# Two layers of a hybrid trunk on one core: layers written out, modulation moved into branch C, output product by tiles, first stage by feature halves

## The chip, the core and the metric

The kernel runs on one core of a Trainium2 chip. The metric is the time of one execution in microseconds (us); lower is better. Engines are named as the profile names them: PE (TensorE, with PEld for its weight loads), DVE (VectorE), ACT (ScalarE), POOL (GpSimd), SP (SyncE, which here only issues DMAs). One run of each kernel is profiled: its span is from the first to the last instruction.

## The reference, cut to what matters

640 tokens (four tiles of 128 latent tokens and one tile of 128 context tokens), 1024 features, two layers. Each layer does

```python
mod_ctx = silu(c_ctx) @ w_mod[l] + b_mod[l]          # for the context tile
mod_lat = silu(c) @ w_mod[l] + b_mod[l]              # for the four latent tiles
shift, scale, gate = split(mod, 3)
u = layer_norm(x) * (1 + scale) + shift
parts = split_columns(u @ w_in)                      # q, k, v, z of A and C, all of B, merge gates
ya, yw, ym = attention A, windowed attention C, two-directional mLSTM B
merged = sum(sigmoid(g_b) * ((y_b * silu(z_b)) @ w_branch[b]) for the 3 branches)
h = alpha * x + gate * (merged @ w_out)
x = layer_norm(h) * ln_g + ln_b
```

All is float32. `mod` depends on the conditioning and the layer alone, not on x.

## The kernel before, in words

**Tiles.** `T` = 5 token tiles, tile 4 (`LT`) is the context. `act_T` holds the modulated input u, features on partitions, as a rounded part (index 0) and a remainder (index 1). Every weight product is three fp32r products (rounded x rounded, rounded x remainder, remainder x rounded), so each of the eight feature blocks of a chunk of 512 output columns costs 3 matmuls of 512 columns for each tile: 24 a tile, 120 a chunk.

**Weights.** A "piece" is two feature blocks of a chunk, 512 KB. SP loads pieces into a ring of three buffers `raw`; POOL writes the rounded part (`tensor_copy`, L654) and the remainder (`tensor_tensor`, L656) into a ring of two buffers `wsp`; PE (`product`, L703) uses a piece for all five tiles, then takes the next. ACT does the rounding of the four pieces of A's z. The table `Pieces` fixes the order, `PsumPlan` which PSUM bank each result takes; an instruction waits for counts of semaphores `bank_full` and `bank_done`.

**A layer.** Both layers are one loop body (`Fori`). It begins with the modulation: `modulation(n, k)` (L688) multiplies two columns `csil` (silu of the two conditionings) by 512 columns of `w_mod`, 8 feature blocks for each of chunks 0 to 3 (0, 1 shift; 2, 3 scale), straight from `raw`. DVE adds the bias (L1442); 16 small transposes put it into columns `modc`. DVE normalises x in `xh` (L1431 to L1447), PE transposes each tile (`xT`, L743), DVE and ACT modulate it (L1468, L1145), ACT rounds (L1149), DVE takes the remainder (L1458, `u_ready`). Then the products kv, A's q, transposes of k, A's z, transposes of q and z, attention A (`for s in range(STEPS)`, a software pipeline over 32 pairs of head and tile), A's merge products, the same for C, then B, and last the transposes of `merged` and the output product. In steps 0 to 15 of C's loop one `modulation` of chunks 4 and 5 (the gate) stands in each step.

**Output.** The output product goes chunk by chunk over all five tiles: half 0 of all tiles, then half 1. For each tile DVE multiplies by the gate (L1934), adds alpha x (L1953), takes statistics (L1959, L1964), subtracts the mean and multiplies by the gain (L1940); POOL makes the reciprocal root (L642); ACT scales (L1396); POOL adds the bias (L671); for tile 4 DVE does the last step (L1970). SP stores the tiles to the outputs, from which the second layer reads them again for its residual.

**The meeting.** At the end of a layer every engine drains and waits (`meet`), SP waits for all stores, clears all semaphores and lets all go on:

```python
                for name in at_end:
                    sp.wait_ge(at_end[name], 1)
                sp.sem_clear(range(bank_full[0].num, at_end["pool"].num + 1))
                sp.wait_ge(stored, 16 * (4 + 6 + T))
```

## Time and profile before

| what | value |
|---|---|
| time, median of 3 runs | 1812.54 us (1806.18 to 1815.93) |
| time of the profiled execution | 1812.43 us |
| its span | 1810.6 us, 21331 instructions |
| granted clock of PE, mean | 0.957 |
| busy: PE, DVE, ACT, POOL | 1632.6, 792.2, 475.8, 611.7 us |
| chain that ended last | PE 76%, DVE 10%, issue 4%, ACT 4%, DMA 2% |

PE is nearly always the engine that the others wait for. The share of busy time by itself says little here, as a slowly running PE is busy too. What is worth reading is where PE is not fed: the page's slices, and the timeline at the start, at the turn between the layers and at the end.

### The profile page before, as it was taken

To read this page: it belongs to the slowest core of one execution; us is meant where nothing else is said; L and a number is where in the kernel's file an instruction comes from. 1 tells how busy PE (TensorE), PEld (TensorE's weight loads), DVE (VectorE), ACT (ScalarE), POOL (GpSimd) and SP (SyncE) were. 2 spreads that over 40 slices of the span, in tenths; PEclk is the share of its full clock that TensorE was granted. 3 is DMA by queue.
4 is the path that set the end of the run, shared out by engine and by line. 5 is a ranking of instruction groups with operands and counts; after the bars stand their busy time and mean duration, and the time that the engine had idled before them with its cause. 6 is when DMAs were issued, how large, how long until landed. Compare 5 with 4: busy or idle time off the path is not lost.

```text
span 1810.6 us, 21331 instructions
## 1 busy us (share of the span) xinstructions
PE 1632.6 (90%) x8235; PEld 1250.8 (69%) x8235; DVE 792.2 (44%) x1456; ACT 475.8 (26%) x1111; POOL 611.7 (34%) x351
## 2 busy tenths in 40 slices
PE   4798899999899999999658979999998999999994
PEld 0487678884588887787505867788746888877874
DVE  2348740356612434323633587304465234252255
ACT  0223740135600133301102237401345001332011
POOL 0254005520044443253512540154210544423535
PEclk8899999998999999999869989999999999999997
DMA  7421002212112222141054310022130222211411
GB/s 259 131 83 58 1 12 71 81 47 85 36 58 82 59 71 64 35 152 59 35 179 128 85 47 1 13 81 78 39 95 26 70 82 59 71 53 47 151 59 58
DMA packets 75874, 131.34 MB, mean 73 GB/s; under 512 B 16044, under 2 KB 20544, under 8 KB 75716
## 3 DMA queue, kind: packets, MB, share of 16 engines
q1 hardware_dynamic: 74728, 124.15, 22.6%
q10 hardware_dynamic: 1040, 5.77, 0.8%
q8 instruction: 68, 1.11, 0.3%
q14 instruction: 38, 0.31, 0.1%
HBM read 123.61 MB, written 8.92 MB: 73 GB/s over the span
## 4 chain that ended last, share of the span: by engine, by line
PE 76%; DVE 10%; issue 4%; ACT 4%; DMA 2%; SPq 2%; POOL 2%; POOLq 0%; ACTq 0%; DVEq 0%
PE pb L718 55%; PE pb L743 4%; PE pb L897 3%; PE pb L696 3%; PE pb L854 2%; DMA raw<-in_w_mod 2%; PE pb L816 2%; PE pb L934 1%; PE pb L827 1%; PE pb L823 1%; DVE rtmp L1553 1%; DVE tokq L1538 1%; SPq L567 1%; POOL rstd L642 1%; POOL xh L671 1%
## 5 line engine op out<-in xcount | busy, mean ns | idle before, releaser
L718 PE MATMUL pb<-wsp,act_T 128*128 128x512 f32 x4080 | 950.3, 393 | 9.2 <-issue 9.2
L718 PEld LDWEIGHTS pb<-wsp,act_T 128*128 128x128 f32 x4080 | 769.5, 189 | 176.9 <-issue 17.2
L654 POOL CAST wsp<-raw 128x1024 fp32r<-128x1024 f32 x152 | 163.0, 1072 | 1102.2 <-PE pb L718 898.2
L656 POOL TENSOR_TENSOR wsp<-raw,wsp 128x1024 fp32r<-128x1024 f32 x160 | 390.6, 2441 | 34.1 <-ACT wsp L1167 21.9
L718 PE MATMUL pb<-wsp,yT 128*128 128x512 f32 x720 | 169.9, 395 | 0.0
L696 PE MATMUL pb<-raw,csil 128*2 128x512 f32 x192 | 104.8, 669 | 59.8 <-DMA raw<-in_w_mod 57.1
L718 PEld LDWEIGHTS pb<-wsp,yT 128*128 128x128 f32 x720 | 135.4, 188 | 32.5
L1914 DVE SCALAR_TENSOR_TENSOR mt<-tg,pb 128x512 f32<-128x512 f32 x40 | 27.4, 685 | 260.2 <-PE pb L718 259.4
L1387 ACT ACTIVATE tg<-pb 128x512 f32<-128x512 f32 x60 | 36.0, 600 | 363.7 <-PE pb L718 363.7
L696 PEld LDWEIGHTS pb<-raw,csil 128*2 128x2 f32 x192 | 12.6, 88 | 122.9 <-DMA raw<-in_w_mod 80.0
L1235 ACT ACTIVATE pr<-pb,nm 128x640 f32<-128x640 f32 (+2 forms) x128 | 91.2, 713 | 2.0 <-DVE nm L1605 2.0
L1914 DVE SCALAR_TENSOR_TENSOR merged<-tg,pb 128x512 f32<-128x512 f32 x20 | 13.7, 687 | 148.8 <-PE pb L718 148.8
L854 PE MATMUL pb<-ident,pr 128*128 128x128 f32 x480 | 74.7, 276 | 1.5 <-ACT pT L1272 1.2
L1635 DVE TENSOR_SCALAR pr<-pr,rden 128x640 f32<-128x640 f32 (+2 forms) x128 | 70.4, 550 | 4.5
L816 PE MATMUL pb<-kT,qT 128*128 128x320 f32 x256 | 56.3, 343 | 9.6 <-ACT prc L1213 7.3
L1605 DVE TENSOR_REDUCE nm<-pb 128x1 f32<-128x640 f32 x64 | 52.5, 820 | 27.3 <-PE pb L816 27.2
L854 PEld LDWEIGHTS pb<-ident,pr 128*128 128x128 f32 x480 | 54.0, 142 | 4.1 <-issue 2.7
L1608 DVE TENSOR_REDUCE nmx<-pb 128x1 f32<-128x384 f32 (+1 forms) x64 | 39.7, 621 | 39.0 <-PE pb L831 38.6
L816 PEld LDWEIGHTS pb<-kT,qT 128*128 128x128 f32 x256 | 39.7, 197 | 21.5 <-issue 9.6
L1918 DVE TENSOR_TENSOR merged<-merged,mt 128x512 f32<-128x512 f32 x40 | 51.5, 1287 | 1.4
L1145 ACT ACTIVATE utmp<-pb,modc 128x128 f32<-128x128 f32 x40 | 15.1, 457 | 119.7 <-PE pb L743 119.1
L1262 ACT COPY pT<-pb 128x512 f32<-128x512 f32 x64 | 37.6, 587 | 31.6 <-PE pb L854 29.7
(242 smaller groups left out, 1637.8 us busy)
## 6 DMA issues: line engine op xcount, KB each, us to landing
raw<-in_w_in SPq DMA_DIRECT2D x112, 512.0 KB, 3.6
raw<-in_w_mod SPq DMA_DIRECT2D x48, 512.0 KB, 4.3
raw<-in_w_branch SPq DMA_DIRECT2D x24, 512.0 KB, 3.5
raw<-in_w_out SPq DMA_DIRECT2D x16, 512.0 KB, 3.5
out<-xh SPq DMA_DIRECT2D x10, 512.0 KB
raw<-in_w_in SPq DMA_DIRECT2D x16, 256.0 KB, 3.3
xh<-out SPq DMA_DIRECT2D x2, 2048.0 KB, 8.7
xh<-in_x_sample ACTq DMA_DIRECT2D x1, 2048.0 KB, 8.6
```

The lines of the kernel that those rows point to most:

```text
L654: pool.tensor_copy(hi, raw[:, p % 3, :, 0:width]).then_inc(pool_step, 1)
L656: pool.tensor_tensor(lo, raw[:, p % 3, :, 0:width], hi.bitcast(F32), ALU.subtract)\
L696: mm = pe.matmul(pb[0:2, psum.bank(key), :], csil[:, k, :], raw[:, p % 3, k % 2, :], start=(k == 0), stop=(k == KD - 1))
L718: mm = pe.matmul(dst, lhs(a, k, t), wsp[:, piece % 2, w, j, 0:width], start=(k == 0 and n == 0), stop=(i == count - 1 and j == 1 and n == 2))
L743: mm = pe.transpose(pb[:, b, tile_cols(i % 4)], src(i), ident[:, :])
L816: mm = pe.matmul(pb[:, b + i, 0:320], q, kT[:, kv, a, i * 320:(i + 1) * 320], start=(a == 0), stop=(a == 1))
L854: mm = pe.transpose(pb[:, psum.bank((br, "PT", s)), tile_cols(i)], pr[:, (s + 2) % 3, tile_cols(i)], ident[:, :])
L897: mm = pe.matmul(pb[r, psum.bank(key), (2 * hh + lo) * P:(2 * hh + hi) * P], v_of, pT[:, g % 2, place_of, 2 * e + lo:2 * e + hi, :] .rearr ...
L1235: act.activation(dst, src, ACT.Exp, bias=nm[:, s % 4:s % 4 + 1], accum_out=lsum[:, s % 4:s % 4 + 1]).then_inc(*done((br, "S", s)))
L1605: dve.tensor_reduce(nm[:, o], pb[:, b:b + 2, 0:320], AX.XY, ALU.max, negate=True)\
L1635: dve.tensor_scalar(p, p, rden[:, o], None, ALU.mult).then_inc(p_ready, 1)
L1918: ins = dve.tensor_tensor(merged[:, t, cs], merged[:, t, cs], mt[:, t % 2, :], ALU.add)
```

## The change

1. The two loop passes are written out, each with its own semaphores; the meeting is gone, and the second layer's work follows the first's on each engine as its own waits allow.
2. Modulation: only chunks 0 to 3 of the first layer are made at the start, from 16 buffers `stage`, loaded by SP and ACT. The other eight chunks stand in branch C's loop: six in the first layer (four of them the second layer's shift and scale), 24 steps with two feature blocks in each; two in the second layer, 8 steps. A block's product is no longer one matmul of 512 columns with 2 stationary columns, but four of 128 columns with 32 stationary columns, each into its own 32 partitions of PSUM; the bias is a product with `ident`. The gate is broadcast from `mrow` by 16 matmuls of 128 columns, before by 4 of 512.
3. The output product is done for tiles 0 to 2 (both halves), then 3 and 4. Its eight pieces, and the second layer's kv and q pieces, stay resident in `slots`. In the first layer DVE normalises each finished tile twice (the layer's own norm, and the next layer's), ACT writes the normalised input into `xn`, PE transposes it, and the next layer's kv and q are multiplied tile by tile, kv of tile t before the transposes of t+1.
4. The first layer's start goes by halves of the features: chunks 0 and 2 give modulation of blocks 0 to 3, then half of kv's product, then chunks 1 and 3, blocks 4 to 7 and the other half.
5. The transposes of k stand inside z's product, behind its third piece. POOL's remainder of a piece is made by two instructions of half the width. In the second layer ACT does the rounding of the four q pieces too.

```diff
+START_CHUNKS = (0, 2, 1, 3)
+LATE_CHUNKS = (((1, 0), (1, 2), (1, 1), (1, 3), (0, 4), (0, 5)), ((1, 4), (1, 5)))
+MOD_FROM = 2
+OUT_SLOTS = (("A1", "A2", "M1", "M2"), ("Y1", "Y2", "w0", "w1"))
+KV_SLOTS = ("T1", "T2", "A1", "A2")
+Q_SLOTS = ("M1", "M2", "w0", "w1")
+Z_SLOTS = ("T1", "T2", "w0", "w1")
+
+OUT_FIRST = (0, 1, 2)
...
+def out_calls(l):
+
+    if l == 0:
+        return [(hf, OUT_FIRST) for hf in range(2)] + [(hf, (3, 4)) for hf in range(2)]
+    return [(hf, OUT_FIRST) for hf in range(2)] + [(hf, (t,)) for t in (3, 4) for hf in range(2)]
...
-            with sp.Fori(0, DEPTH) as l:
...
+            for l in range(DEPTH):
+                here[0] = l
...
-                for name in at_end:
-                    sp.wait_ge(at_end[name], 1)
-                sp.sem_clear(range(bank_full[0].num, at_end["pool"].num + 1))
-                sp.wait_ge(stored, 16 * (4 + 6 + T))
-                sp.sem_clear(stored)
-                sp.drain().then_inc(go_on, 1)
...
+                    load_stage(0)
+                    for p in range(3):
+                        load_piece(p)
+                    load_stage(2)
+                    load_small(0)
...
+                for j in range(2):
+                    ins = pool.tensor_tensor(lo[:, j, :], raw[:, p % 3, j, 0:width], hi[:, j, :].bitcast(F32), ALU.subtract)
+                ins.then_inc(raw_used, 1)
...
+            kv, q, z = chunk(1, "kv"), chunk(1, "A", "q"), chunk(1, "A", "z")
+            split(kv[0])
+            split(kv[1])
+            of_out(0, 0)
+            split(kv[2])
+            of_next(1, 0)
+            of_out(0, 1)
+            split(kv[3])
+            of_next(1, 1)
+            of_out(0, 2)
+            split(q[0])
+            of_next(1, 2)
+            split(q[1])
...
-                    mm = pe.matmul(pb[0:2, psum.bank(key), :], csil[:, k, :], raw[:, p % 3, k % 2, :],
-                                   start=(k == 0), stop=(k == KD - 1))
-                    if k == KD - 1:
-                        mm.then_inc(*full(key))
-                    elif k % 2:
-                        mm.then_inc(mod_used, 1)
...
+                def modulation(b, k, src):
+
+
+                    for q in range(4):
+                        mm = pe.matmul(pb[32 * q:32 * q + 32, b, 0:P], csil[:, k, :], src[:, tile_cols(q)],
+                                       start=(k == 0), stop=False)
+                    return mm
...
-                for n in range(4):
-                    for k in range(KD):
-                        modulation(n, k)
-                acquire("modT")
-                for n in range(4):
-                    wait_done(pe, ("mod", n))
-                for i in range(2 * KD):
-                    mm = pe.transpose(pb[:, 6, 2 * i:2 * i + 2], modrow[:, tile_cols(i)], ident[0:2, 0:2])
-                mm.then_inc(*full("modT"))
-
-                for t in range(T):
-                    pe.wait_ge(xn_ready, t + 1)
-                    transpose_blocks(("xT", t), lambda i: xh[:, t, tile_cols(i)], KD)
-
-
-                project(("kv",), tile_ready=lambda t: pe.wait_ge(u_ready, t + 1))
...
+                    start_chunk(0)
+                    pe.wait_ge(xn_ready[0], T)
+                    for k in range(4):
+                        turn_input(k)
+                    start_chunk(1)
+                    turn_chunk(("modT", 0), 0)
+                    turn_chunk(("modT", 1), 1)
+                    project(("kv",), part=(0, 1), tile_ready=lambda t: inputs_ready(0))
+                    start_chunk(2)
+                    start_chunk(3)
+                    turn_chunk(("modT", 2), 2)
+                    turn_chunk(("modT", 3), 3)
+                    for k in range(4, 8):
+                        turn_input(k)
+                    project(("kv",), part=(2, 3), tile_ready=lambda t: inputs_ready(1))
+                    project(("A", "q"))
...
+                    project((br, "z"), after=keys)
...
-                        if br == "C" and s < 2 * KD:
-                            modulation(4 + s // KD, s % KD)
+                        if br == "C":
+                            late_step(s)
...
-                    project(("out", hf), tile_ready=(lambda t: wait_done(pe, ("mT", t))) if hf == 0 else None)
-                meet(pe, "pe", l)
...
+                def turn_next(t):
+                    pe.wait_ge(xn_ready[here[0]], t + 1)
+                    transpose_blocks(("xT", t), lambda i: xn[:, tile_cols(i)], KD)
+
+                def first_turned(i, t):
+                    if (l, i, t) == (0, 2, T - 1):
+                        here[0] = l + 1
+                        turn_next(0)
+                        here[0] = l
+
+                calls = out_calls(l)
+                for n, (hf, tiles) in enumerate(calls):
+                    project(("out", hf), tiles=tiles, tile_ready=(lambda t: wait_done(pe, ("mT", t))) if hf == 0 else None,
+                            after=first_turned if n == len(calls) - 1 else None)
+                if l + 1 < DEPTH:
+                    here[0] = l + 1
+                    for t in range(T):
+                        project(("kv",), tiles=(t,), by_tile=True, tile_ready=lambda t: pe.wait_ge(u_ready[1], t + 1))
+                        if t + 1 < T:
+                            turn_next(t + 1)
+                        project(("A", "q"), tiles=(t,), by_tile=True)
...
+                    normalised(0)
+                    hi_piece(q)
+                    hi_piece(q + 1)
+                    modulated(0)
+                    normalised(1)
+                    hi_piece(q + 2)
+                    hi_piece(q + 3)
+                    of_kv(0)
+                    modulated(1)
...
+                def mean(t):
+
+                    dve.wait_ge(dve_step[l], ends[1, t])
+                    step(dve.bn_aggr(out=mv[:, t, :], in_=stats[:, t, :, :].rearrange("p a b -> p (a b)")))
+                    dve.tensor_scalar(ve[:, t:t + 1], mv[:, t, 1:2], EPS, None, ALU.add).then_inc(ln_var[l], 1)
                     dve.scalar_tensor_tensor(out=xh[:, t, :], in0=xh[:, t, :], scalar=mv[:, t, 0:1],
                                              in1=lnrow[:, 0, :], op0=ALU.subtract, op1=ALU.mult)\
-                        .then_inc(centred, 1)
-
-
-                for i in range(4):
-                    wait_done(dve, ("gate", i))
-                order = [(hf, t) for hf in range(2) for t in range(T)]
-                aggregated = 0
-                gated(*order[0])
-                for n, (hf, t) in enumerate(order):
-                    cs = slice(hf * HALF, (hf + 1) * HALF)
-                    wait_done(dve, ("out", hf, t))
-                    added = marked(dve.scalar_tensor_tensor(out=xh[:, t, cs], in0=xh[:, t, cs], scalar=ALPHA,
-                                                            in1=ot[:, t % 2, :], op0=ALU.mult, op1=ALU.add))
-                    if hf and t:
-                        dve.wait_ge(dve_step, aggregated)
-                        centre(t - 1)
-                    dve.wait_ge(dve_step, added)
-                    counted = marked(dve.bn_stats(out=stats[:, t, hf, :], in_=xh[:, t, cs]))
-                    if n + 1 < len(order):
-                        gated(*order[n + 1])
-                    if hf:
-                        dve.wait_ge(dve_step, counted)
-                        aggregated = marked(dve.bn_aggr(out=mv[:, t, :],
-                                                        in_=stats[:, t, :, :].rearrange("p a b -> p (a b)")))
-                dve.wait_ge(dve_step, aggregated)
-                centre(LT)
-                dve.wait_ge(rstd_ready, 3 + T + LT)
-                dve.wait_ge(centred, T)
-                dve.scalar_tensor_tensor(out=xh[:, LT, :], in0=xh[:, LT, :], scalar=rstd[:, LT:LT + 1],
-                                         in1=lnrow[:, 1, :], op0=ALU.mult, op1=ALU.add).then_inc(context_ready, 1)
-                meet(dve, "dve", l)
+                        .then_inc(centred[l], 1)
+
+                def scaled(t):
+
+                    dve.wait_ge(ln_rstd[l], t + 1)
+                    dve.wait_ge(centred[l], t + 1)
+                    dve.scalar_tensor_tensor(out=xh[:, t, :], in0=xh[:, t, :], scalar=rstd[:, t:t + 1],
+                                             in1=lnrow[:, 1, :], op0=ALU.mult, op1=ALU.add).then_inc(x1_ready[l], 1)
+
+                def next_mean(t):
+
+                    dve.wait_ge(x1_ready[l], t + 1)
+                    for i in range(2):
+                        ins = dve.bn_stats(out=stats2[:, t, i, :], in_=xh[:, t, i * HALF:(i + 1) * HALF])
+                    step(ins)
+                    step(dve.bn_aggr(out=mv2[:, t, :], in_=stats2[:, t, :, :].rearrange("p a b -> p (a b)")))
+                    dve.tensor_scalar(ve2[:, t:t + 1], mv2[:, t, 1:2], EPS, None, ALU.add).then_inc(xn_var[1], 1)
+
+                def next_shift(t):
+                    dve.wait_ge(xn_rstd[1], t + 1)
+                    dve.scalar_tensor_tensor(out=nmr[:, t:t + 1], in0=mv2[:, t, 0:1], scalar=-1.0,
+                                             in1=rstd2[:, t:t + 1], op0=ALU.mult, op1=ALU.mult).then_inc(next_ready[1], 1)
+
+                def modulated(t):
+                    w = 1 if t == LT else 0
+                    wait_full(dve, ("xT", t), 1)
+                    if t >= 2:
+                        dve.wait_ge(u_ready[1], t - 1)
+                    src = pb[:, use(("xT", t), 1)[0]:use(("xT", t), 1)[0] + 2, :].rearrange("p b (n i) -> p (b n) i", i=P)
+                    for k in range(KD // 2):
+                        ins = dve.tensor_scalar(utmp[t % 2][:, k, :], src[:, k, :], modc[:, KD + k, w:w + 1],
+                                                modc[:, k, w:w + 1], ALU.mult, ALU.add)
+                    ins.then_inc(u_half[1], 1)
+
+                def remainder(t):
+                    wait_done(dve, ("xT", t), 1)
+                    dve.tensor_tensor(act_T[:, 1, :, tile_cols(t)], utmp[t % 2][:, :, :],
+                                      act_T[:, 0, :, tile_cols(t)].bitcast(F32), ALU.subtract).then_inc(u_ready[1], 1)
...
```

The first place is PE at the turn between the layers. Before, the transposes of `merged` and all of the output product end the loop body (the 240 matmuls are both halves), and behind them PE leaves the pass by way of the meeting (L511):

```order
L718 MATMUL pb<-wsp,yT 128x512 x60
L743 MATMUL pb<-ident,merged 128x128 x40
L718 MATMUL pb<-wsp,act_T 128x512 x240
L511 REGISTER_ALU
L682 REGISTER_ALU
L682 COMPARE_AND_BRANCH
```

Now the end of the first layer's output product (tiles 3 and 4, half 1), the transposes of the first normalised tile, and kv, the next transposes and q of the second layer, tile by tile:

```order
L942 MATMUL pb<-slot_Y_137,act_T 128x512 x12
L942 MATMUL pb<-slot_Y_138,act_T 128x512 x12
L942 MATMUL pb<-wsp,act_T 128x512 x12
L967 MATMUL pb<-ident,xn 128x128 x8
L942 MATMUL pb<-wsp,act_T 128x512 x12
L942 MATMUL pb<-slot_T_131,act_T 128x512 x6
L942 MATMUL pb<-slot_T_132,act_T 128x512 x6
L942 MATMUL pb<-slot_A_133,act_T 128x512 x6
L942 MATMUL pb<-slot_A_134,act_T 128x512 x6
L967 MATMUL pb<-ident,xn 128x128 x8
L942 MATMUL pb<-slot_M_135,act_T 128x512 x6
L942 MATMUL pb<-slot_M_136,act_T 128x512 x6
```

The modulation is gone from this place, and the products of the second layer stand directly behind the first's.

The second place is DVE from the statistics of tile 2 on, in the same stretch: what stands between the third tile's statistics and the first remainder (L2438) that kv of tile 0 waits for.

```order
L2422 SCALAR_TENSOR_TENSOR nmr<-mv_77,rstd_79 128x1
L2415 BN_STATS stats_76<-xh 128x6 x2
L2417 BN_AGGR mv_77<-stats_76 128x2
L2418 TENSOR_SCALAR ve_78<-mv_77 128x1
L2385 TENSOR_TENSOR ot<-pb,gate_bc 128x512 x2
L2391 SCALAR_TENSOR_TENSOR xh<-xh,ot 128x512
L2393 BN_STATS stats<-xh 128x6
L2391 SCALAR_TENSOR_TENSOR xh<-xh,ot 128x512
L2393 BN_STATS stats<-xh 128x6
L2422 SCALAR_TENSOR_TENSOR nmr<-mv_77,rstd_79 128x1
L2432 TENSOR_SCALAR utmp_129<-pb,modc 128x128 x4
L2438 TENSOR_TENSOR act_T<-utmp_129,act_T 128x8x128
```

Before, nothing of the next layer stood in this stretch; the last rows of a layer were

```order
L1959 BN_STATS stats<-xh 128x6
L1964 BN_AGGR mv<-stats 128x2
L1939 TENSOR_SCALAR ve<-mv 128x1
L1940 SCALAR_TENSOR_TENSOR xh<-xh,mv,lnrow 128x1024
L1970 SCALAR_TENSOR_TENSOR xh<-xh,rstd,lnrow 128x1024
```

What moved is that the modulation of tile 0 now stands behind the next norm's statistics of tiles 0 to 2 and behind half 0 of tiles 3 and 4.

The third place is PE inside branch C of the first layer, two steps near the loop's start; `raw,csil` and `bmod,ident` are the modulation's products. Before:

```order
L823 MATMUL pb<-kT,qT 128x128 x2
L827 MATMUL pb<-kT,qT 128x384 x2
L831 MATMUL pb<-masks 128x128 x2
L854 MATMUL pb<-ident,pr 128x128 x4
L696 MATMUL pb<-raw,csil 2x512
L823 MATMUL pb<-kT,qT 128x128 x2
L827 MATMUL pb<-kT,qT 128x256 x2
L831 MATMUL pb<-masks 128x128
L854 MATMUL pb<-ident,pr 128x128 x3
L696 MATMUL pb<-raw,csil 2x512
```

Now:

```order
L1092 MATMUL pb<-kT,qT 128x128 x2
L1096 MATMUL pb<-kT,qT 128x384 x2
L1100 MATMUL pb<-masks 128x128 x2
L1123 MATMUL pb<-ident,pr 128x128 x4
L898 MATMUL pb<-raw,csil 32x128 x8
L1092 MATMUL pb<-kT,qT 128x128 x2
L1096 MATMUL pb<-kT,qT 128x256 x2
L1100 MATMUL pb<-masks 128x128
L1123 MATMUL pb<-ident,pr 128x128 x3
L898 MATMUL pb<-raw,csil 32x128 x8
L905 MATMUL pb<-bmod,ident 32x128 x4
```

Each product of 512 columns (one feature block a step) has become four of 128 columns, eight a step (two blocks), and a chunk ends with four more for its bias.

## Rows read from the trace of the kernel before

**Rows 1.** Waits of PE over the span: us in total, times, longest.
```profile
...
PE pb L696 <- DMA raw<-in_w_mod: 57.1, 17, 30.9
PE pb L743 <- DVE zt L1567: 13.5, 2, 6.8
...
```

**Rows 2.** Timeline: both output products, kv of the second layer: start us, us.
```profile
...
834.25 55.98 PE L718 MATMUL pb<-wsp,act_T 128*128 128x512 f32 x238 [0.67 <-issue]
...
977.96 2.47 PE L718 MATMUL pb<-wsp,act_T 128*128 128x512 f32 x5 [4.16 <-issue]
...
1733.26 54.68 PE L718 MATMUL pb<-wsp,act_T 128*128 128x512 f32 x240 [0.77 <-issue]
...
```

**Rows 3.** Timeline behind the last output product of the first layer: start us, us, engine.
```profile
...
885.29 0.69 DVE L1934 TENSOR_TENSOR ot<-pb,gate_bc 128x512 f32<-128x512 f32 x1 [14.48 <-PE pb L718]
886.01 0.69 DVE L1953 SCALAR_TENSOR_TENSOR xh<-xh,ot 128x512 f32<-128x512 f32 x1
886.74 0.69 DVE L1959 BATCH_NORM_STATS2 stats<-xh 128x6 f32<-128x512 f32 x1
...
887.94 0.20 DVE L1964 BATCH_NORM_AGGREGATE mv<-stats 128x2 f32<-128x12 f32 x1
...
888.67 0.14 DVE L1939 TENSOR_SCALAR ve<-mv 128x1 f32<-128x1 f32 x1
888.73 1.27 DVE L1940 SCALAR_TENSOR_TENSOR xh<-xh,mv,lnrow 128x1024 f32<-128x1024 f32 x1
...
892.07 1.53 POOL L642 TENSOR_TENSOR rstd<-ve,half_neg 128x1 f32<-128x1 f32 x1 [1.66 <-DVE ve L1939]
...
893.57 2.34 POOL L671 TENSOR_TENSOR xh<-xh,lnrow 128x1024 f32<-128x1024 f32 x1
...
894.41 2.05 DVE L1953 SCALAR_TENSOR_TENSOR xh<-xh,ot 128x512 f32<-128x512 f32 x1
...
916.56 6.03 DVE L1431 BATCH_NORM_STATS2 stats<-xh 128x6 f32<-128x512 f32 x10 [6.71 <-issue]
...
972.74 1.06 PE L743 MATMUL pb<-ident,xh 128*128 128x128 f32 x8 [1.00 <-ACT act_T L1149]
...
977.89 1.37 DVE L1468 TENSOR_SCALAR utmp<-pb,modc 128x128 f32<-128x128 f32 x4
...
979.17 1.22 DVE L1458 TENSOR_TENSOR act_T<-utmp,act_T 128x1024 fp32r<-128x1024 f32 x1
979.42 1.05 ACT L1149 CAST act_T<-utmp 128x1024 fp32r<-128x1024 f32 x1
```

**Rows 4.** Chain that ended last, end of the second layer.
```profile
...
1803.75 3.35 DVE xh L1970
```

**Rows 5.** Timeline: ACT reads the last kv tile of the first layer.
```profile
...
105.26 0.37 ACT L1154 COPY kvt<-pb 128x256 f32<-128x256 f32 x1 [0.71 <-PE pb L718]
...
```

**Rows 6.** Busy times by stretch, at the start and late in branch C.
```profile
...
40.00:45.00 5.00, 4.09 (x10) 0.74 (x11) 0.57 (x2) 0.00 (x0) 0.00 (x0) 1.00 0.88 283
...
475.00:485.00 10.00, 8.38 (x69) 6.14 (x68) 8.19 (x29) 7.81 (x24) 0.00 (x0) 1.00 0.00 0
...
```

**Rows 7.** Timeline of PE inside branch C.
```profile
...
420.87 1.09 PE L863 MATMUL pb<-pTc,kv 128*64 128x128 f32 x16
421.89 1.02 PE L696 MATMUL pb<-raw,csil 128*2 128x512 f32 x2
...
```

**Rows 8.** Page, part 5: the costliest groups, GpSimd's.
```profile
...
L654 POOL CAST wsp<-raw 128x1024 fp32r<-128x1024 f32 x152 | 163.0, 1072 | 1102.2 <-PE pb L718 898.2
L656 POOL TENSOR_TENSOR wsp<-raw,wsp 128x1024 fp32r<-128x1024 f32 x160 | 390.6, 2441 | 34.1 <-ACT wsp L1167 21.9
...
```

**Rows 9.** Page, part 6: DMA issues.
```profile
...
raw<-in_w_mod SPq DMA_DIRECT2D x48, 512.0 KB, 4.3
...
```

**Rows 10.** Page, part 3: DMA queues.
```profile
...
q8 instruction: 68, 1.11, 0.3%
q14 instruction: 38, 0.31, 0.1%
...
```

1494 lines of the change are left out of this document (953 added, 541 removed).

## Prediction

> **What bounds the kernel now.** I read the waits of PE first. Of all its waits one stands out: 57.1 us for `w_mod`, in the two modulation stages; the next, 13.5 us, is for the gating of z [rows 1]. So elsewhere PE is fed, and time can come only from the stages without weight products and from a change in PE's own work. How long the first kind is, the timeline shows, once one sees where PE's product ends: DVE begins with tile 0 of the last half at 885.29, but PE still has four tiles to go. The first layer's output product runs from 834.25 for 55.98 us, to 890.2, and kv of the second layer starts at 977.96 [rows 2]: 87.7 us, in which PE makes only modulation and transposes. The second output product ends at 1733.26 + 54.68 = 1787.9 [rows 2], the last DVE step at 1807.1 [rows 4], and the span at 1810.6: 22.7 us. At the start the last tile of kv is read at 105.26 [rows 5]; what is left, two layers of some 800 us of dense work, the change mostly keeps.
>
> **Turn.** Removed: meeting, reload of x, modulation, all 87.7 us. Added to PE at this place: only the transposes of five tiles, 5 x 1.06 = 5.3 us, already there before [rows 3]. The question is how long PE waits for DVE. I lay it out from the start of the output product. A matmul takes 54.68/240 = 0.228 us [rows 2], 24 take 5.5. In half 1, tiles 0 to 2 are done at 30.1, 31.4 and 32.8 us, all at 54.7. From 30.1 DVE has, up to the first remainder (the order above): 5 gate products at 0.69, 5 additions and 5 statistics at 0.69 each, 3 means (0.20 + 0.14 + 1.27), 3 final scalings at 1.27, 3 next statistics (2 x 0.60, from 6.03/10, + 0.34), shifts 0.4, half a modulation 1.37, ACT's rounding 1.05, remainder 1.22 [rows 3]. That is 3.5 + 6.9 + 4.8 + 3.8 + 4.6 + 0.4 + 1.4 + 1.1 + 1.2 = 27.7 us, so u of tile 0 at 57.8. Two things come on top. POOL's roots take 1.53 us, and that for tile 2 stands behind the next layer's root of tile 1: 2 x 1.53 with hand-overs, 4.5 us of waiting. And DVE is held while POOL works: `xh<-xh,ot` takes 2.05 instead of 0.69 when it starts behind POOL's 2.34 us addition [rows 3]. POOL's splits (1.07 + 2.44 a piece [rows 8]), now with a half-width remainder, stand among DVE's steps: two for kv, two for q before tile 0 is ready, 1 us each: 4 us. So u(0) at 66.3 against PE free at 54.7: 12 us (bounds: 3 if nothing is held; 20 if every one of the 11 steps with two inputs in SBUF is held 1.2 us). The Trainium skill, "SBUF — State Buffer" (Who interferes with whom), has the port shared by DVE and GpSimd as an exclusive lock for a whole instruction; the trace agrees with its 2.05 us.
>
> For tile 1 DVE has 1.4 + 2.8 + 3.2 + 1.3 + 1.5 + 1.4 + 1.1 + 1.2 = 13.9 us, with 2 us held 16, while PE has kv, transposes and q of tile 0, 5.5 + 1.1 + 5.5 = 12: 4 us more. Later tiles need less than 12 each. A restart after a stall at half clock I put at 2 us. New gap 5.3 + 12 + 4 + 2 = 23; saved **64.7 us** (bounds 53 to 79).
>
> The weights don't stop PE: eight output pieces are used in 33 us, 4.1 each, POOL needs 3.5 each [rows 8], and the third must be there 8 us after the merged transposes and is at 3.5.
>
> **End.** The last tile has 0.69 + 0.69 + 0.69 + 0.20 + 0.14, POOL 1.53, DVE 1.27 [rows 3] (POOL is idle otherwise; the addition of the mean's step runs beside the root), and from DVE's end to the span's end 3.5 us as now: 8.8 in place of 22.7. Earlier tiles are through, since tile 3 is 11 us older. Saved **13.9** (bounds 10 to 15).
>
> **Start.** x, chunks 0 and 2 and the tables are about 7 MB on two queues (with what else they load). Loads ran at 283 GB/s [rows 6]; 25 us with 2 us of issue. DVE waits there for the tables before it normalises, five tiles 4 us (29.5); transposes 2.6, chunk 2's products 4, columns 1.5 (38); four blocks of features, DVE and ACT alternating over 640 tokens, 6.5 (44.5); half of kv 13.5 (58); chunks 1 and 3 8.5, columns 1.5, features 8 (76); the other half of kv 13.5: 89.5. Now 105.3. Saved **15** (bounds 5 and 28, if the loads come 10 us later or the features are hidden behind the chunks).
>
> **Branch C.** A block costs PE 0.95 us now (1.02 with the end of its pipeline [rows 7]), and I take it as bare: it stands between the steps' other products, and PE waits for nothing there. Of the new form, 32 stationary columns, no row stands here; the nearest are eight f32 products of 128 columns with 64 stationary columns, alternately into two halves of PSUM: 1.02 us, 0.128 each [rows 7], half of a quarter of 0.95. So two neighbours overlap. A block is then 4 x 0.128 = 0.51. First layer: 24 steps x 1.02 + six biases 0.5 + four transposes = 28 us, in place of 16 x 0.95 = 15.2; of it some 4 us hide in steps 16 to 25, where PE was busy only 8.38 of 10 us [rows 6]: +9. Second layer: 8 x 1.02 + 1 - 15.2 = -6, half a microsecond taken back as the steps are then set by others. Together **+3.5** with rounding up (bounds: quarters wholly overlapped, 0.24 a block, -13; not at all, +25). By the Trainium skill, "TensorEngine Tiling (Array Packing)" (Theoretical Speedup), a product with at most 32 columns could gain up to four times; by it the sum would be some 17 us lower. It adds (Key Properties) that a change of mode drains the engine; the 1.02 us for eight products shows no sign of it. The loads need 4.3 us from issue to landing [rows 9]; with three buffers that is 1.5 us a piece against steps of over 2, so they stay hidden. The gate's broadcast has the same columns as before: nothing.
>
> **z in the second layer.** The 6.8 us wait of each layer [rows 1] stays in the first. In the second DVE begins A's q early, but k waits for POOL's root behind a split that waits for q's last piece; I see it ready as the third piece of z ends. Saved **5** of 6.8 (bounds -3 and 7).
>
> Sum, against the profiled execution's own 1812.43 (the median is 1812.54, the same): 1812.4 - 64.7 - 13.9 - 15 + 3.5 - 5 = **1717**.
>
> **Rivals.** (a) The forecast, 1717, its own range 1695 to 1740: 0.70. (b) The quarters don't overlap, or drain the engine each time: 0.95 a block, so 21 + 7 us in C and 14 at the start: 1717 + 42 = 1759. For it: no row has 32 columns; against it: rows 7. 0.08. (c) The turn becomes DVE's: if held steps double their time, each of the five tiles needs some 20 us of DVE against 12 of PE: four times 8 more, 1749. For it: 2.05 for 0.69; against: POOL splits only eight pieces there. 0.12. (d) Better on every side, quarters overlapped and DVE not held: 1717 - 17 - 12 = 1688. 0.07. (e) Slower: written out, the program has no loop to come back to, and instructions must be fetched for each pass. There are 68 + 38 packets of instructions [rows 10]; if each stopped its engine and the others with it, the break-even of 95 us comes at 0.9 us a packet, and at 2 us the time is 1717 + 212 = 1929. Against: 1.42 MB is 67 bytes for each of 21331 instructions, so both passes are fetched already, and PE's waits show no such gap. 0.03, of which a third comes out about level.
>
> **Numbers.** The likeliest is 1717. The range 1688 to 1757 holds (a), (c) and (d). A run of this kernel can tell about 0.5% from no change. Faster by more: 0.97; within: 0.01; slower: 0.02.
>
> **What would show it.** In the profile of the changed kernel: kv's last tile read near 90; no meeting, and 20 to 25 us between the last output product and the last of kv's first tile without a dense PE, most of it before tile 0, waiting for DVE's remainder (L2438); the quarter products in pairs of 0.13; DVE steps of 1.3 to 2 us at the turn beside POOL; 9 us from the last product to the end. Wrong would be: waits of PE on `raw<-in_w_mod` in C's loop, or 1.9 us for eight products; a wait for `k_ready` inside z of more than 5 us; gaps of PE marked issue all over the span.

## Result and the profile after

The changed kernel takes 1695.5 us (median of 4, 1694.6 to 1696.8) against 1813.9 us for the kernel before, timed beside it (1806.2 to 1815.9): a ratio of 0.936, 95% interval 0.934 to 0.938. The profiled execution has a span of 1693.8 us, 116.8 less than before; 95.1 were forecast.

First where the time went. Both kernels do the same weight products in the same order, so the stages can be cut at the same products: the first product with `yT` of branches A and C and the first output product of each layer. Each length is the difference of two starts on PE's timeline. The experiments' stages stand beside them, since most verdicts are read there.

```
us                to A's    A to C   C to out  out to A's  A to C   C to out  out to
                  first yT  layer 1  layer 1   yT, layer 2 layer 2  layer 2   end
before             283.8     241.5    309.0     350.9       238.5    309.6     77.3
after              269.1     234.8    306.6     283.8       226.4    309.0     64.2
e1 turn order      268.1     234.4    306.6     281.5       226.0    309.0     64.2
e2 k root          268.0     234.7    306.6     285.1       225.5    308.9     64.2
e3 start whole     262.3     234.8    306.6     284.7       225.7    308.9     64.2
e4 POOL full       268.4     236.9    308.4     285.1       228.8    309.2     64.3
e5 serial          267.7     270.9    308.1     284.7       236.9    307.4     64.2
e6 double          268.1     247.2    308.2     284.3       229.1    309.0     64.3
e7 POOL quiet      268.8     234.7    306.6     274.8       225.7    309.0     64.2
e8 all tiles       268.9     234.7    306.6     299.2       227.0    307.4     64.3
e9 turn both       269.5     235.0    306.6     273.0       226.6    307.3     64.3
e10 k early        267.2     234.7    306.6     288.6       225.8    309.0     64.3
e11 POOL quarters  267.2     234.4    306.3     279.4       225.1    308.7     64.2
e12 together       257.0     234.5    306.3     268.5       225.1    308.7     64.2
```

A stage that an edit doesn't touch still differs from run to run: the start by 2.3 us (267.2 in e10 to 269.5 in e9), C of the second layer by 1.5 (225.5 in e2, 227.0 in e8), C to out by 1.6 (308.2 in e6; 307.4 and 309.0 in the second layer). Smaller differences in one stage show nothing.

After against before: 14.7 at the start, 67.1 at the turn, 13.1 at the end, 6.7 and 12.1 in the two stages with branch C, 3.1 in the rest. The first three were forecast; in C's stages the forecast had 3.5 us more, not 18.8 less.

The page of the changed kernel, parts 1 and 3 (as of before, which had 68 + 38 packets of instructions [rows 10]):

```profile
span 1693.8 us, 22318 instructions
...
PE 1563.2 (92%) x8931; PEld 1260.8 (74%) x8931; DVE 757.9 (45%) x1468; ACT 472.2 (28%) x1099; POOL 628.4 (37%) x504
...
q8 instruction: 71, 1.16, 0.3%
q14 instruction: 32, 0.26, 0.1%
```

71 + 32 packets: the program written out is fetched no more often than the loop.

PE's timeline at the turn (start us, us, and in brackets the idle time before), which answers to [rows 2] and the transposes of [rows 3]:

```profile
810.44 8.67 PE L942 MATMUL pb<-slot_A,act_T 128*128 128x512 f32 x36 [1.29 <-issue]
...
863.13 1.04 PE L967 MATMUL pb<-ident,xn 128*128 128x128 f32 x8
863.92 2.99 PE L942 MATMUL pb<-wsp,act_T 128*128 128x512 f32 x12
878.24 4.58 PE L942 MATMUL pb<-slot_T,act_T 128*128 128x512 f32 x12 [11.33 <-DVE act_T L2438]
882.66 2.97 PE L942 MATMUL pb<-slot_A,act_T 128*128 128x512 f32 x12
...
894.38 4.58 PE L942 MATMUL pb<-slot_T,act_T 128*128 128x512 f32 x12 [2.42 <-DVE act_T L2438]
...
940.25 2.88 PE L942 MATMUL pb<-wsp,act_T 128*128 128x512 f32 x12
```

The output product starts at 810.4 and q of the last tile ends at 943.0: 132.5 us, of which 54.7 are output products and as much kv and q (240 + 240 at 0.228 us). 23.1 us are lost, where before 87.7 were; the forecast was 23. It shows how too: 11.3 us for the remainder of tile 0, 2.4 for tile 1, twice a group of products at half clock, 4.58 for 2.97 us, and 5.2 of transposes; the last 1.0 is mostly the output product, which here too takes 0.9 more than before.

DVE and GpSimd while PE waits:

```profile
848.40 0.15 DVE L2399 TENSOR_SCALAR ve<-mv 128x1 f32<-128x1 f32 x1
848.47 2.28 DVE L2400 SCALAR_TENSOR_TENSOR xh<-xh,mv,lnrow 128x1024 f32<-128x1024 f32 x1
...
858.24 2.31 DVE L2408 SCALAR_TENSOR_TENSOR xh<-xh,rstd,lnrow 128x1024 f32<-128x1024 f32 x1
...
864.43 3.49 POOL L798 TENSOR_TENSOR slot_M<-raw,slot_M 128x512 fp32r<-128x512 f32 x2
864.50 2.30 DVE L2408 SCALAR_TENSOR_TENSOR xh<-xh,rstd,lnrow 128x1024 f32<-128x1024 f32 x1 [1.16 <-POOL rstd L784]
...
866.73 1.22 DVE L2422 SCALAR_TENSOR_TENSOR nmr<-mv,rstd 128x1 f32<-128x1 f32 x1
...
876.87 1.23 DVE L2438 TENSOR_TENSOR act_T<-utmp,act_T 128x1024 fp32r<-128x1024 f32 x1 [1.17 <-ACT act_T L1753]
```

The scaling of 1.27 us takes 2.3 wherever GpSimd's subtraction runs, and the step on one column takes 1.22 instead of 0.15. Over the nine lengthened steps from 841 to 878 us that is 7.9 us (one of them, 1.91 for 1.27, began beside GpSimd's copy L795). Waiting for roots is rare: 1.2 us here.

In branch C, a step of the first layer (its answer is [rows 7]):

```profile
405.38 0.65 PE L898 MATMUL pb<-raw,csil 128*32 128x128 f32 x16
405.96 0.44 PE L1092 MATMUL pb<-kT,qT 128*128 128x128 f32 x2
```

Sixteen records are eight products, two feature blocks, and the next product begins 0.58 us later. Before, one block cost 0.95. The granted clock differs as well. Windows of 5 us late in C's loop, in the kernel before (busy us of PE, PEld, DVE, ACT and POOL, then the granted clock, DMA share, GB/s):

```profile
490.00:495.00 5.00, 5.00 (x22) 2.17 (x16) 1.38 (x2) 2.28 (x4) 0.00 (x0) 0.83 0.00 0
495.00:500.00 5.00, 5.00 (x12) 3.18 (x11) 0.00 (x0) 0.59 (x1) 0.00 (x0) 0.50 0.00 0
```

and the last two windows of the same stretch after:

```profile
471.00:476.00 5.00, 4.74 (x43) 4.07 (x44) 1.39 (x2) 1.99 (x5) 0.00 (x0) 1.00 0.00 0
476.00:481.00 5.00, 5.00 (x27) 4.21 (x27) 0.00 (x0) 1.08 (x2) 0.00 (x0) 1.00 0.01 3
```

What PE did there, before and after: the broadcast of the gate, then the 120 weight products up to the stage's end.

```profile
491.02 5.00 PE L771 MATMUL pb<-grow,ident 2*128 2x512 f32 x8
495.95 29.45 PE L718 MATMUL pb<-wsp,act_T 128*128 128x512 f32 x120
```

```profile
472.92 3.84 PE L1014 MATMUL pb<-mrow,ident 128*128 128x128 f32 x32
476.52 27.50 PE L942 MATMUL pb<-wsp,act_T 128*128 128x512 f32 x120
```

Before, PE was granted half of full speed, 1.2 GHz, from some 2 us into the broadcast (four products over two rows) on, and went into the weight products with it; after, the grant stays at 2.4 GHz. The modulation's products are not what stood there: the last of them began at 452.6, and from 440 to 460 us the grant was 1.00. No run tried why it fell.

The end: the last product ends at 1685.2 and the span at 1693.8, 8.6 us (22.7 before, 8.8 forecast). The start: ACT reads the last kv tile at 90.26 (105.26 [rows 5]; 89.5 forecast).

### The profile page after: what moved, and what is told of

The parts are those of the page before. It is cut to its first block, busy times and chain, and to the rows that moved or that the text cites. A ratio compares the mean times of both kernels' runs of the same rounds, so it can differ in the third digit from the quotient of the medians.

```text
span 1693.8 us, 22318 instructions
## 1 busy us (share of the span) xinstructions
PE 1563.2 (92%) x8931; PEld 1260.8 (74%) x8931; DVE 757.9 (45%) x1468; ACT 472.2 (28%) x1099; POOL 628.4 (37%) x504
## 4 chain that ended last, share of the span: by engine, by line
PE 79%; DVE 11%; ACT 3%; issue 3%; POOL 1%; ACTq 1%; POOLq 0%; DVEq 0%
PE pb L942 58%; PE pb L1166 4%; PE pb L967 3%; PE pb L1123 2%; PE pb L1085 2%; PE pb L898 1%; PE pb L1203 1%; PE pb L1092 1%; PE pb L1096 1%; DVE xh L2400 1%; ACTq L1405 1%; DVE xh L2408 1%; ACT prc L1547 1%; PE pb L1340 1%; PE pb L1117 1%
## 5 line engine op out<-in xcount | busy, mean ns | idle before, releaser
L942 PE MATMUL pb<-wsp,act_T 128*128 128x512 f32 x3480 | 813.8, 393 | 11.7 <-DVE act_T L1862 11.7
L942 PEld LDWEIGHTS pb<-wsp,act_T 128*128 128x128 f32 x3480 | 655.4, 189 | 152.2 <-issue 16.4
L795 POOL CAST wsp<-raw 128x1024 fp32r<-128x1024 f32 x132 | 145.3, 1101 | 894.0 <-PE pb L942 755.8
L798 POOL TENSOR_TENSOR wsp<-raw,wsp 128x512 fp32r<-128x512 f32 x280 | 371.7, 1348 | 24.5 <-ACT wsp L1432 13.9
L942 PE MATMUL pb<-slot_A,act_T 128*128 128x512 f32 x180 | 43.9, 397 | 2.6 <-issue 2.6
L942 PE MATMUL pb<-slot_T,act_T 128*128 128x512 f32 x120 | 32.3, 428 | 13.7 <-DVE act_T L2438 13.7
L784 POOL TENSOR_TENSOR rstd<-ve,half_neg 128x1 f32<-128x1 f32 (+1 forms) x16 | 16.4, 1035 | 74.8 <-DVE ve L2399 35.5
L942 PE MATMUL pb<-slot_M,act_T 128*128 128x512 f32 x180 | 42.9, 392 | 0.0
```

The source lines that it names most:

```text
L795: pool.tensor_copy(hi, raw[:, p % 3, :, 0:width]).then_inc(raw_hi, 1)
L798: ins = pool.tensor_tensor(lo[:, j, :], raw[:, p % 3, j, 0:width], hi[:, j, :].bitcast(F32), ALU.subtract)
L942: mm = pe.matmul(dst, lhs(a, k, t), w[:, wa, j, 0:width], start=(k == 0 and n == 0), stop=(i == count - 1 and j == 1 and n == 2))
```

## Experiments

All twelve are edits of the changed kernel; its 1695.5 us (span 1693.8) is what they stand against. Intervals are those of the ratio to the kernel before, which ran beside each group of experiments: 1808.7 to 1812.6 us, where it took 1813.9 beside the changed kernel. The ratios give sizes up to 2 us away from those of the times (e9 8.3 us less for 10.2, e11 6.5 for 8.5), so differences below 2 us say nothing.

**C: what the quarters are worth (e5, e6).** My theory after the result: four products in four quarters of the array run at a time.

```diff
-                        mm = pe.matmul(pb[32 * q:32 * q + 32, b, 0:P], csil[:, k, :], src[:, tile_cols(q)],
-                                       start=(k == 0), stop=False)
+                        dst = pb[0:32, b, tile_cols(q)] if late[0] else pb[32 * q:32 * q + 32, b, 0:P]
+                        mm = pe.matmul(dst, csil[:, k, :], src[:, tile_cols(q)],
+                                       start=(k == 0 and (q == 0 or not late[0])), stop=False)
```

> The changed kernel with the late modulation of branch C in one quarter of the array: the four products of a feature block, 32 stationary and 128 moving columns each as before, all write partitions 0 to 31, side by side in the bank's 512 columns. DVE still reads what it read, so the gate and the second layer's modulation hold other values. In the changed kernel a step's 8 products (two blocks) take 0.57 us, where the prediction had 1.02. Theory: a quarter's product is as long as before and four run at a time; in one quarter they must follow each other, 0.95 a block as the 512-column product of before, 1.33 us more in each of 32 steps, some 40 us: 1735 to 1740, less some us hidden where C's steps wait for ACT. Rival: the short products themselves are cheap (0.07 us each), whichever quarter they use: 1695.

1741.9 us (0.962, 0.960 to 0.965), 46.3 more, 2 above the foreseen range and far from the rival's 1695. A step of e5 and, below it, one of e6:

```profile
403.32 1.93 PE L900 MATMUL pb<-raw,csil 128*32 128x128 f32 x16
405.18 0.44 PE L1096 MATMUL pb<-kT,qT 128*128 128x128 f32 x2
```

Same columns, same count, 1.86 us for 0.58: what made them cheap was the four quarters. 32 x 1.28 = 41 us, and the eight bias groups (0.95 for 0.35) are 5: that is the whole difference. The shown cause of C's gain is the overlap.

```diff
+                        for j in range(2):
+                            mm = modulation(bank_of(key), 2 * i + j, raw[:, p % 3, j, :], again=True)
```

> The changed kernel with each late step's eight quarter products issued twice (the sums are then twice what they should be in the gate and the second layer's modulation); loads unchanged. Theory: PE is bare in those 32 steps, so 32 x 0.57 = 18.3 us more: 1712 to 1714. Rival: C's steps are set by DVE and ACT with room on PE, and most of it is hidden: under 1701.

```profile
402.90 1.08 PE L898 MATMUL pb<-raw,csil 128*32 128x128 f32 x32
403.91 0.44 PE L1094 MATMUL pb<-kT,qT 128*128 128x128 f32 x2
```

1710.7 us (0.944, 0.942 to 0.947): 15.2 more, 12.4 in the first layer's C stage (24 steps, 0.52 each) and 2.8 in the second's (8 steps, 0.35). That is 3 us under the theory and far over the rival: PE is nearly bare there, as the prediction took it. A second set of eight adds 0.43 us, not 0.58: 0.215 a block, and 0.15 us once for the whole group. Whether the 0.15 is paid on entering or on leaving, the rows don't tell.

**GpSimd's instruction length (e4, e11, e7).** The change also cut GpSimd's remainder of a piece into two instructions (L798), to which the prediction gave nothing outside the turn.

```diff
-                for j in range(2):
-                    ins = pool.tensor_tensor(lo[:, j, :], raw[:, p % 3, j, 0:width], hi[:, j, :].bitcast(F32), ALU.subtract)
-                ins.then_inc(raw_used, 1)
+                pool.tensor_tensor(lo, raw[:, p % 3, :, 0:width], hi.bitcast(F32), ALU.subtract).then_inc(raw_used, 1)
```

> The changed kernel with GpSimd's remainder of a piece in one instruction of 1024 columns again, not two of 512, everywhere. In the changed kernel ten DVE steps between 841 and 878 us take 7.9 us more than the same steps elsewhere (2.3 for 1.27, 1.2 for 0.15). Theory: DVE is held for the rest of a running GpSimd instruction, so with instructions of 2.4 us each held step loses up to 1.2 us more: the wait for tile 0 grows by 3 to 6 us, the rest of the program, fed by PE, doesn't move: 1699 to 1702. Rival: what DVE loses is set by GpSimd's total busy time, not by the length of an instruction: within 1.5 us of 1695.5.

1702.8 us (0.939, 0.936 to 0.942): 7.2 more, but the five runs spread from 1698.2 to 1704.8, 2.7 to 9.3 more. All are slower than every run of the changed kernel, so the rival is out; the size, foreseen as 3 to 6, is loose. The places are other ones than foreseen: 1.3 at the turn, 2.1 and 2.4 in the stages with C, where attention's DVE steps are held and PE waits for them through ACT (for `pT` 4.2 us in the first layer's C, 2.9 in the changed kernel). In the second layer's C these waits grow by about 1 us; there the longest, 2.4 us for 1.5, is followed by products at half clock, and the grant over the loop is 0.93 for 0.96. The 1.8 in the first layer's C to out show nothing: e5 and e6, which leave GpSimd alone, have 1.5 and 1.6 there.

```diff
+                    for a in (slice(0, width // 2), slice(width // 2, width)):
+                        ins = pool.tensor_tensor(lo[:, j, a], raw[:, p % 3, j, a], hi[:, j, a].bitcast(F32), ALU.subtract)
```

> The changed kernel with GpSimd's remainder in four instructions of 256 columns, not two of 512. One of 1024 cost 7.2 us (1702.75). Its trace: turn and second layer's kv 1.3 us more, the attention stages and the recurrence between them 6. Theory: what DVE loses to a running GpSimd instruction goes with its length, so another halving gives back half of that: 3 to 4 us, 1692. Rival: DVE is then held more often for shorter times, or GpSimd's overhead of two more instructions eats it: within 1.5 us of 1695.5, or slower.

1687.0 us (0.932, 0.930 to 0.934): 8.5 less, more than twice what was expected. 4.4 are at the turn. The 1.3 in the second layer's C and the 1.8 at the start are no more than runs differ by: e10, unchanged at the start, has the same 267.2. DVE's scaling of tile 1 (L2408 in the changed kernel) with GpSimd's subtraction whole, in quarters, and nearly absent (e7):

```profile
861.50 3.42 DVE L2406 SCALAR_TENSOR_TENSOR xh<-xh,rstd,lnrow 128x1024 f32<-128x1024 f32 x1
```

```profile
854.58 1.75 DVE L2409 SCALAR_TENSOR_TENSOR xh<-xh,rstd,lnrow 128x1024 f32<-128x1024 f32 x1
```

```profile
855.78 1.27 DVE L2410 SCALAR_TENSOR_TENSOR xh<-xh,rstd,lnrow 128x1024 f32<-128x1024 f32 x1
```

3.42, 2.31, 1.75 and 1.27 us for the same step: beyond its own 1.27 it waits 2.15, 1.04 and 0.48 us, for GpSimd instructions of 2.43, 1.35 and 0.80 us (means of part 5). That quartering cost GpSimd 66 us of busy time (694 for 628) and still won says that length, not total time, is what DVE pays. By the Trainium skill, "SBUF — State Buffer" (Who interferes with whom), the shared port pair is an exclusive lock; the trace agrees, with 0.6 to 0.9 of one GpSimd instruction for each hold. That DVE waits once for each of its instructions, and not for all of GpSimd's work, is these runs' finding.

```diff
+                n = 8 if p in turn_pieces else width
...
-                                mm = pe.matmul(dst, lhs(a, k, t), w[:, wa, j, 0:width],
+                                mm = pe.matmul(dst, lhs(a, k, t), w[:, 0 if p in turn_pieces else wa, j, 0:width],
```

> The changed kernel with GpSimd's remainders of the eight pieces of kv and q of the second layer cut to 8 of 512 columns; PE multiplies with the rounded part in their place (the products' count and shape stay, the small correction is lost). GpSimd then does almost nothing but roots at the turn. Theory (the prediction's, with the size that the trace now gives): ten held DVE steps lose 7.9 us there, so the wait for tile 0 falls from 11.3 to 3 or 4 us: 1687 to 1688. Rival: the wait is made by the roots and the order of the steps, DVE then idles for them, and less than 3 us is gained.

1685.2 us (0.931, 0.928 to 0.933): 10.4 less. PE's wait for tile 0 is 4.2 us, for tile 1 0.3. Holding cost 7 us of the first wait; the theory holds, with 2 us more than foreseen. The roots also come sooner when the remainders in front of them are short, but in the changed kernel DVE waited for a root only 1.2 us, so that explains little.

**The turn (e8, e1, e9).**

```diff
-        return [(hf, OUT_FIRST) for hf in range(2)] + [(hf, (3, 4)) for hf in range(2)]
+        return [(hf, tuple(range(T))) for hf in range(2)]
```

> The changed kernel with the first layer's output product over all five tiles, half after half, as before the change, and DVE's and PE's orders fitted to it (first halves of tiles 3 and 4 early; tile 0's transposes behind the product). Tile 0 of the second half is then done 49 us behind the start of the product, not 30. From there DVE has 32 us of steps in its order until the first remainder, so u(0) at 81 in place of 67.8 us: 10 to 14 us longer, 1706 to 1709. Rival: the chain for one tile alone is only some 15 us, and what DVE did early is off it: within 3 us.

1710.8 us (0.945, 0.942 to 0.948), 15.3 more: PE waits 16.2 us for tile 0's normalised input and 10.2 for its remainder. That is 1 to 5 us more than foreseen. So of the turn's 64 us some 15 come from the order by tiles; that the other 50 come from the meeting, reload and modulation that are gone is what the subtraction leaves, no run has it alone.

```diff
                     next_mean(1)
+                    modulated(0)
                     scaled(2)
-                    next_shift(1)
-                    next_mean(2)
                     gated(0, 3)
+                    remainder(0)
+                    next_shift(1)
                     gated(0, 4)
+                    next_mean(2)
                     added(0, 3)
+                    modulated(1)
+                    remainder(1)
                     added(0, 4)
                     next_shift(2)
-                    modulated(0)
-                    remainder(0)
...
```

> The changed kernel with DVE's order at the turn altered: the modulation and remainder of tile 0 come ahead of the additions for tiles 3 and 4, those of tile 1 ahead of the second halves of tiles 3 and 4. My theory: PE's 11.3 us wait for the remainder of tile 0 is a matter of order, since DVE finished next_shift(0) at 861.7 and got to the remainder at 876.9, with 13 us of work for tiles 2 to 4 between, and it has idle time again from 898 on (4.6, 6.6 and 2.8 us). Then the wait falls to about 2 us, the 2.4 us for tile 1 to about 0, and the two half-clock products (4.58 us in place of 2.97) are gone: 9 + 2 + 3 = 14 us less, 1681 us. Rival: the turn is bound by DVE's total work; the wait goes from tile 0 to tiles 1 to 3 and the time stays within 3 us of 1695.5.

1693.4 us (0.934, 0.932 to 0.937): 2 less, not 14. The time is the rival's, but not its way: the new wait is for GpSimd. The theory held for DVE and failed for the sum:

```profile
867.81 3.05 PE L942 MATMUL pb<-slot_T,act_T 128*128 128x512 f32 x12 [2.26 <-DVE act_T L2438]
...
887.15 2.93 PE L942 MATMUL pb<-wsp,act_T 128*128 128x512 f32 x6 [8.49 <-POOL wsp L798]
```

The wait for tile 0 went from 11.3 to 2.3 us and a new one of 8.5 came for the split of q's last piece. GpSimd has it behind the root of tile 3 (`of_out(0, 3)`), which started at 883.04, when DVE's mean was there. It was late before too, but hidden in the longer wait.

```diff
             split(q[2])
-            of_out(0, 3)
             split(q[3])
+            of_out(0, 3)
```

> The reordered turn of the first experiment, and GpSimd's split of q's last piece ahead of its root for tile 3. There DVE's remainder of tile 0 came at 867.8 as foreseen and PE's wait for it fell from 11.3 to 2.3 us, but PE then waited 8.5 us for the split of q's last piece: GpSimd had it behind the root of tile 3, for which DVE's mean came at 883.0. Theory: that wait and its half-clock products go, 8 to 10 us less than 1693.4: 1684 to 1685. Rival: tile 3's root is late instead, DVE comes to tile 3 too late, and PE waits as long there.

1685.3 us (0.931, 0.929 to 0.933): 8 less than e1, 10.2 less than the changed kernel. PE now waits 2.3, 1.4 and 1.0 us.

**The start (e3).** Taken out: the two calls of kv by feature halves, in their place one behind all chunks.

```diff
-                    project(("kv",), part=(0, 1), tile_ready=lambda t: inputs_ready(0))
...
-                    project(("kv",), part=(2, 3), tile_ready=lambda t: inputs_ready(1))
+                    project(("kv",), tile_ready=lambda t: inputs_ready(1))
```

> The changed kernel without the feature halves on PE: chunks 1 and 3 of the modulation and the other four feature blocks come ahead of kv, which then runs in one piece; the loads, ACT's and DVE's orders are the same. The prediction credited the start's 15 us partly to half of kv hiding the second half's loads. In the trace the loads run at 370 to 400 GB/s and are over at about 40 us, before the first half of kv begins at 43.4. Theory: the halves hide nothing; PE idles 7.7 and 4.0 us in both forms, the second features come 16 us earlier, and kv ends some 5 us earlier: 1690 to 1692. Rival (the prediction's): the halves are worth their time, as PE has nothing in the second features' 8 to 10 us: kv ends 4 to 10 us later, 1700 to 1705.

1688.5 us (0.932, 0.929 to 0.934): 7.0 less, where the theory had 4 to 5 and the rival a loss. The last tile of kv is read at 84.23, not 90.26:

```profile
55.02 40.28 PE L942 MATMUL pb<-wsp,act_T 128*128 128x512 f32 x169 [4.07 <-DVE act_T L1861]
...
84.23 0.37 ACT L1439 COPY kvt<-pb 128x256 f32<-128x256 f32 x1 [0.71 <-PE pb L942]
```

The loads run at 374 GB/s from 20 to 35 us and are over by 40, before kv could begin (43.4). The halves hid no load; they cost 6 us of what the start had to give.

**k of the second layer (e2, e10).**

```diff
             of_q(1, 3)
+            of_kv(1)
             split(z[2])
-            of_kv(1)
```

> The changed kernel with GpSimd's root for k of the second layer put ahead of the split of z's third piece, not behind it. In the changed kernel DVE waits 4.9 us for that root and PE 2.9 + 2.5 us for the keys inside z. Theory: the root is what k waits for, so DVE's wait goes and PE's falls to about 1 us: 4 us less, 1691 to 1692. Rival: then z's third piece is late by as much (PE waits for wsp or slot instead), or DVE's own k path of some 13 us is what is late: no change.

1695.0 us (0.936, 0.933 to 0.938): no change, the theory falls. DVE's wait for the root was 2.4 us in place of 4.9, PE's waits 2.6 + 2.7 in place of 2.9 + 2.5: ACT rounds the keys behind q's tile 3.

```diff
+                        k_rounded()
                         q_rounded(br, 3)
-                        k_rounded()
...
+                        k_lo(br)
                         q_path(br, 3)
                         q_lo(br, 2)
                         q_squares(4)
-                        k_lo(br)
```

> The changed kernel with k of the second layer ahead of q's tile 3 in both queues: ACT rounds the keys before that tile, DVE makes their remainders right behind its k path. With the earlier root (second experiment) DVE got the root 1.5 us sooner and PE's waits stayed at 2.6 + 2.7 us, since ACT's rounding stood behind tile 3. Theory: keys are ready at 963.5 against PE's 964, both waits go: 4 to 5 us less, 1690.5 to 1691.5. Rival: q's tile 3 is late in turn and PE waits for it as long at the transposes.

1700.7 us (0.939, 0.937 to 0.941): 5.2 slower, neither theory. The keys were ready in time, and PE then waited for their copies out of PSUM:

```profile
973.59 2.79 PE L967 MATMUL pb<-ident,ks 128*128 128x128 f32 x12 [10.31 <-ACT kT L1506]
```

These stand on ACT behind q's tile 4, for which ACT waited 6.4 us: DVE's new order made its root later, and DVE itself stood 1.8 us waiting for it. One queue's head had been moved and the rest of it left.

**All that paid (e12).** The edits of e3, e9 and e11, and k ahead of q's tile 3 with the copies ahead too:

```diff
+                        k_rounded()
+                        k_turned()
                         q_rounded(br, 3)
-                        k_rounded()
                         q_rounded(br, 4)
-                        k_turned()
```

> The changed kernel with four edits at once: kv of the first stage in one piece behind all four chunks (third experiment, 7.0 us), the reordered turn with GpSimd's split ahead of tile 3's root (ninth, 10.2 us), GpSimd's remainder in four instructions (eleventh, 8.5 us), and k of the second layer ahead of q's tile 3, this time with ACT's copies of the turned keys ahead of q's tiles 3 and 4 too: in the tenth experiment PE waited 10.3 us for those copies, which stood behind a q tile whose root came late. Theory: start 7 and turn 10 add up; the quarters' 8.5 us lie half in the turn (the wait for tile 0 there was 7.7 for 11.3 us), which has only 2.3 us of it left, so 3 or 4 more; PE's 5.7 us of waits for keys go down to 1: 1670 to 1673. Rival: the copies still wait for something, no gain at k: 1675 to 1678. If the quarters held their full gain beside the new turn: 1667.

1667.9 us (0.921, 0.919 to 0.923): 27.6 less than the changed kernel, 2 to 5 less than expected, and next to the third case, 1667, in which the quarters keep their full gain. At the keys PE waits no more:

```profile
932.99 6.99 PE L943 MATMUL pb<-wsp,act_T 128*128 128x512 f32 x30
939.82 2.97 PE L968 MATMUL pb<-ident,ks 128*128 128x128 f32 x24
...
953.28 1.06 PE L968 MATMUL pb<-ident,tokq 128*128 128x128 f32 x8 [3.66 <-DVE zt L2006]
```

The next wait is the gating of z, 3.7 us. The stage from the output product to A's `yT` is 268.5 us against 273.0 with e9 alone; how these 4.5 divide between quarters and k was not tried apart. The start, 257.0, is 5.3 under e3's; runs differ by 2.3 there without cause, and the rest I have not traced.

## Why the forecast was right, and where not

The time, 1695.5 us, lies in the range, 21.5 below the likeliest 1717 and at the lower edge of the forecast's own 1695 to 1740. The three stages that were to save time did so almost to the microsecond, in part by luck; the sum for branch C had the wrong sign.

1. **Turn.** Forecast 64.7 saved (new gap 23), measured 87.7 - 23.1 = 64.6. Its parts: wait for tile 0 11.3 (12 forecast), tile 1 2.4 (4), half clock 3.2 (2), transposes 5.2 (5.3), and 0.9 for a slower output product that nothing had foreseen. Inside the first, two errors cancelled: "4 us" of held steps were 7.9, and 4.5 us of waiting for roots were 1.2 where it showed. That is luck; e7 confirms the holding and its size.
2. **End.** 13.9 forecast, 14.1 measured from the last product to the end of the span. The last stage as a whole gained 13.1, since the output product itself took 55.6 us, 0.9 more than before. No run tried the end by itself.
3. **Start.** 15 forecast; 15.0 measured at kv's last tile. The stations fit as well: half of kv begins at 43.4 (44.5 forecast), the other half at 73.6 (76). Two things were off and partly cancelled: the loads, taken at 283 GB/s, came at 374, and the first half of kv took 16.4 us for 13.5, as it began at half clock. That the halves themselves are a loss of 6 to 7, as e3 shows, stood in no rival.
4. **Branch C.** The step that failed: "half of a quarter of 0.95. So two neighbours overlap. A block is then 4 x 0.128 = 0.51." It was 0.29 a block. With it the forecast's own formula gives, for the first layer, 24 x 0.58 + 2.1 for six biases + 1.0 for four transposes - 15.2 - 4 = -2.2, and for the second 8 x 0.58 + 0.7 - 15.2 + 0.5 = -9.4: -11.6 where +3.5 stood. The row chosen was of 64 stationary columns, which leaves room for two; I read from it that two overlap, and carried the number of two over to a form with room for four. The same error took the other end: -13 for "wholly overlapped" would have been nearly right. The bound for "not at all", +25, was added up wrongly besides: the same formula gives 24 x 1.90 + 3.5 - 19.2 + 1.5 = +31, as rival (b) has it with its 28 above the forecast; in e5 C's two stages take 28 more than before the change. The Trainium skill, "TensorEngine Tiling (Array Packing)" (Theoretical Speedup), has up to four times for at most 32 columns, from which the prediction estimated 17 us less; the trace agrees: 64 records in a run, eight blocks, take 1.95 us, 0.244 a block against 0.95, 3.9 times, and 0.29 inside the loop.
5. **What was left at nothing.** In C's stages three things. GpSimd's halved subtraction: e4 has 4.5 us more there. The gate's broadcast, "nothing" for having the same columns: to the next weight product it took 4.93 and 3.88 us in the two layers, and takes 3.60 in both, 1.6 less. The 120 weight products behind the loop: 29.3 and 28.7 us, now 27.3 in both, 3.3 less, as they began at half clock before. With point 4 these make -21.0 where -18.8 was measured, so one of the parts, the 4 us taken as hidden or e4's share perhaps, is 2.2 too large; none but the quarters and GpSimd's halves was tried by itself. The stages behind C gained 3.1: from the first transposes of `merged` to the output product PE takes 7.0 us in each layer, before 9.7 and 10.3. It waited 3.15 us for DVE's L1925 there and now waits 0.71; DVE's additions to `merged` then ran beside GpSimd's split (2.14 for 0.69 us), which now comes behind the transposes. Against these 6.0 stands B in the second layer, 2.6 longer, with a granted clock of 0.91 from 1460 to 1480 us. e4 shows nothing for these stages.
6. **z of the second layer.** "Saved 5 of 6.8" was wrong: PE waits 2.9 + 2.5 us for the keys instead, so 1.4 were saved; in sum that passes the 5 us that were named as a sign of being wrong. I had looked at k's root alone; e2 and e10 show three things in line behind it, the rounding, the remainders and the copies, each behind a tile of q.
7. **Rivals.** The time lies between the forecast and rival (d), 1688, nearer to (d), but for half its reason: the quarters overlapped, DVE was held. (e), slow instruction fetch, is out by 71 + 32 packets in place of 68 + 38 and by issue gaps of 3% of the chain, 4% before. (b) is out by e5, (c) by waits of 11.3 and 2.4 us and none of that size for later tiles.

By terms: C came out 22.3 us better than forecast, 15.1 of them the quarters' size, and the stages behind it 3.1 better. Against that stand 2.6 in the turn's stage, 0.8 at the end and 0.3 at the start: 21.7 better in all. The 2.6 are in the main z's 3.6, less 1.4 that the forecast hadn't counted: before, the second layer's first 240 products began at half clock too and took 56.1 us (977.96 to 1034.09), not 54.7.
